# Twenty-four low-half subtracts of weights move from GpSimd to DVE

## The reference, cut to what matters

```
h    = rms_norm(x) ; proj = h @ w_in
y0   = compressed / selected / window attention      (from proj)
y1   = stick-breaking attention                      (from proj)
y2   = gated linear attention, 4 heads               (from proj)
y3   = forgetting attention: softmax(q k^T + cum_q - cum_k), 8 heads, from fox_q, fox_k, fox_v
x    = x + (sum_n sigmoid(gates_n) * (y_n @ w_branch_n)) @ w_out
x    = x + relu(rms_norm(x) @ w_ff1)^2 @ w_ff2
```

## Time and profile before

| | |
|---|---|
| median of 3 runs | 3802.38 us |
| lowest and highest | 3798.88 and 3803.84 us |
| profiled execution, its own time | 3799.13 us |
| span of its profile | 3797.8 us |
| TensorE matmul busy | 3651.8 us (96%) |
| DVE busy | 2161.4 us (57%) |
| ScalarE busy | 1305.7 us (34%) |
| GpSimd busy | 1197.6 us (32%) |
| mean granted TensorE clock | 0.978 |

### The profile page before, as it was taken

How to read it: one execution, slowest core, us unless ns; L and a number is a source line. 1 busy time by engine, 2 the same in 40 slices (tenths; PEclk the granted TensorE clock), 3 DMA queues, 4 the chain that set the end, 5 groups by cost and what they waited for, 6 DMA issues and landing times.

```text
span 3797.8 us, 44671 instructions
## 1 busy us (share of the span) xinstructions
PE 3651.8 (96%) x17862; PEld 2808.5 (74%) x17862; DVE 2161.4 (57%) x3054; ACT 1305.7 (34%) x2217; POOL 1197.6 (32%) x486
## 2 busy tenths in 40 slices
PE   8889999998999999999999999999999999999998
PEld 6646888865588888676777678887767777778887
DVE  7787565688754474633374485545553255365445
ACT  6344121443522131544423532123354433342212
POOL 0002444200144443132333244444213232334443
PEclk9889999997999999999999999999999999999999
DMA  4101333320033333121222123334112222223332
GB/s 135 43 12 50 98 96 95 93 68 12 23 95 99 95 119 107 39 68 56 78 62 78 51 90 99 95 98 148 51 40 78 57 78 61 67 73 95 99 95 83
DMA packets 81373, 292.38 MB, mean 77 GB/s; under 512 B 9712, under 2 KB 11152, under 8 KB 80656
## 3 DMA queue, kind: packets, MB, share of 16 engines
q1 hardware_dynamic: 78384, 278.49, 24.0%
q10 hardware_dynamic: 2784, 11.03, 0.9%
HBM read 285.30 MB, written 2.10 MB: 76 GB/s over the span
## 4 chain that ended last, share of the span: by engine, by line
PE 85%; DVE 11%; issue 2%; ACT 2%; DMA 0%; SPq 0%; DVEq 0%; ACTq 0%
PE acc L334 23%; PE acc L336 22%; PE acc L335 22%; PE banks L929 2%; PE banks L648 2%; PE banks L604 2%; DVE conv_c L1307 2%; PE banks L631 2%; PE banks L940 1%; DVE stat L728 1%; PE banks L1555 1%; DVE probs L739 1%; DVE QK L857 1%; DVE w_lo L247 1%; DVE pair L406 1%
## 5 line engine op out<-in xcount | busy, mean ns | idle before, releaser
L278 POOL TENSOR_TENSOR w_lo<-w_raw,w_hi 128x1024 fp32r<-128x1024 f32 x482 | 1197.4, 2485 | 2570.1 <-ACT w_hi L231 2570.1
L231 ACT ACTIVATE w_hi<-w_raw 128x1024 fp32r<-128x1024 f32 x518 | 548.9, 1060 | 1725.5 <-PE acc L336 1641.6
L334 PE MATMUL acc<-hH,w_hi 128*128 128x512 f32 x1776 | 730.9, 412 | 13.2 <-DVE sig L1940 6.6
L336 PE MATMUL acc<-hL,w_hi 128*128 128x512 f32 x1776 | 699.4, 394 | 0.0
L335 PE MATMUL acc<-hH,w_lo 128*128 128x512 f32 x1776 | 698.8, 393 | 0.0
L334 PEld LDWEIGHTS acc<-hH,w_hi 128*128 128x128 f32 x1776 | 337.9, 190 | 99.7 <-issue 25.3
L334 PE MATMUL acc<-H,w_hi 128*128 128x512 f32 x1024 | 400.4, 391 | 3.8 <-DVE L L398 3.8
L369 DVE TENSOR_TENSOR xT<-acc,xT 128x512 f32<-128x512 f32 x160 | 110.7, 692 | 514.1 <-PE acc L336 495.6
L334 PE MATMUL acc<-midH,w_hi 128*128 128x512 f32 x1024 | 400.3, 391 | 0.3
L335 PE MATMUL acc<-midH,w_lo 128*128 128x512 f32 x1024 | 398.5, 389 | 0.0
L336 PE MATMUL acc<-midL,w_hi 128*128 128x512 f32 x1024 | 398.5, 389 | 0.0
(11 more groups left out here) (325 smaller groups left out, 4710.7 us busy)
## 6 DMA issues: line engine op xcount, KB each, us to landing
w_raw<-in_stream SPq DMA_DIRECT2D x518, 512.0 KB, 3.6
cw<-in_cmpw ACTq DMA_DIRECT2D x2, 2048.0 KB, 7.4
mixed<-in_cmpw ACTq DMA_DIRECT2D x2, 2048.0 KB, 12.7
x_tok<-in_x SPq DMA_DIRECT2D x2, 1024.0 KB, 7.4
out<-f_tok SPq DMA_DIRECT2D x8, 256.0 KB, 2.1
stack<-Z ACTq DMA_DIRECT2D x8, 128.0 KB, 2.3
stack<-Z ACTq DMA_DIRECT2D x8, 127.8 KB, 2.4
masks_f<-in_masks SPq DMA_DIRECT2D x1, 960.0 KB, 12.0
```

The costliest lines, as they stand in the source:

```text
L231: act.activation(w_hi[:, u % WB, 0:w], w_raw[:, u % 2, 0:w], ACT.Copy).then_inc(hi_split, 1)
L278: pool.tensor_tensor(w_lo[:, u % WB, 0:w], w_raw[:, u % 2, 0:w], w_hi[:, u % WB, 0:w], ALU.subtract)\
L334: pe.matmul(acc[n % 2][:, :], wh, H[:, k, :], start=(k == 0), stop=False)
L336: last = pe.matmul(acc[n % 2][:, :], wh, Lo[:, k, :], start=False, stop=(k == nk - 1))
```

## The change

DVE makes the low parts of the units of `fox_in` too, where the index `j` is 2 or more. In `evacuate`, the subtract is issued only behind the last tile of a unit.

```diff
         def by_dve(u):
-            layer, j, group, _, _, _ = UNITS[u]
-            return layer < DEPTH and j >= 2 and group in ("first_in", "late_in")
+            _, j, group, _, _, _ = UNITS[u]
+            return group in ("first_in", "late_in", "fox_in") and j >= 2
...
                 for _ in range(len(self.tiles) if count is None else min(count, len(self.tiles))):
-                    u, _, n = self.tiles.pop(0)
+                    u, t, n = self.tiles.pop(0)
                     dve.wait_ge(acc_ready[n % 2], n // 2 + 1)
                     take(n - self.first, acc[n % 2], acc_free[n % 2], n // 2 + 1)
-                    if u + 2 < len(UNITS) and by_dve(u + 2):
+                    if t == UNITS[u][4] - 1 and u + 2 < len(UNITS) and by_dve(u + 2):
                         split_lo_dve(u + 2)
```

## The result

The changed kernel takes 3807.82 us (median of 22 runs, 3801.50 to 3812.01) against 3801.62 for the kernel before on the same chip. The ratio is 1.0015, 95% interval 1.0009 to 1.0022: by that ratio some 5.7 us slower. The forecast was 3801.6 us, no measurable change, with a range up to 3807.0. It was wrong: the kernel is slower, clear of the noise, and its time lies above the range. The profiled execution took 3808.49 us.

A forecast was written before the change was run, and what follows sets the result against it. TensorE, with 85% of the chain, was taken as the bound, so DVE's work counts only where TensorE waits. 2 x (-0.7 + 0.7 - 0.4 + 0) = -0.8 us from the median 3802.38 gave 3801.6 us, range 3796.5 to 3807.

The forecast's parts named there:

- Bound and mechanism: Around fox_in, TensorE bounds the chain; its idle stretches end with DVE instructions, some held about 2 us by GpSimd's subtracts.
- Term 1: Steady steps behind evacuations: DVE's added subtract fits the slack of 0.71 and 0.32 us before L929, so 0.
- term 5: Late in the fox_in stage: unit 11's DVE subtract overlaps GpSimd's first `mix2` subtract before QK; taken as 0, +1.0 otherwise.
- The steps' rival: Steps behind evacuations lose their slack if DVE's subtract takes 1.9 us or more; 3817.6 us at 2.41; chance 0.05.
- Term 2: Start of the fox_in stage: first L929 comes sooner, limited by unit 3's later load and ScalarE's copy; -0.7 us a layer.
- Term 3: End of run 0: the subtract delays masked copy L885, which TensorE's value matmuls wait for; +0.7 us a layer.
- a new slow stretch: Before the value matmuls, 2.1 us idle lowers TensorE's clock, 1.7 us a layer on top; 3805.0 us; chance 0.15.
- Term 4: Behind the copies of two heads: subtract adds 1.21 us, the gap no longer held saves 1.65; -0.4 us a layer.
- slow stretch with term 5 against me: Lower TensorE clock behind the value matmuls' wait, plus QK held by GpSimd late in the stage: 3807.0 us.

The follow-up runs named there:

- run 0: Not a follow-up kernel: a part of the recurrence within the fox_in stage of each second-type layer, ending with masked copy L885 and TensorE's value matmuls; no time of its own.

## Why the prediction was wrong

**Bound and mechanism: right.** The hold-ups of DVE were GpSimd's subtracts, and went with them. All twelve units of a layer moved, as the index said. The DVE subtract took 1.21 us.

**Term 1, the steady steps: right.** Apart from the meeting of term 5, no idle time stands before the L929 behind an evacuation in the steady steps, in either layer: the slack of 0.71 and 0.32 us held. The steps' rival is out.

**Term 2, the front: right in mechanism, a little low in size.** -0.7 us was forecast for the first L929. It starts at 1913.80 with the stage 1.0 us late, against 1913.92: -1.1; over the six layers of three profiles it is -0.7 to -1.1. The load, ScalarE's copy and the exponentials were the chain, each within 0.7 us of the forecast. The idle time before it is 2.5 to 3.0 us where 3.2 was forecast. Behind it, a slow stretch follows in all six layers of the changed kernel, in four of six of the kernel before, so that part of the gain is paid back. Whether the change causes that difference is open.

**Term 3, the end of run 0: right as a delay, wrong as a whole.** This is the step that failed. It was priced at the delay itself, +0.7 us, and measured +0.6; but the rival "a new slow stretch", held at 0.15, is what happened. The idle time of 2.0 us lay between the 1.41 that the trace showed to be harmless and the 2.44 that it showed to be dear, and I put it with the harmless. It costs 2.2 us a layer by the profile, 4.4 in all; 4.9 to 6.8 by the ratios of the pairs with and without it. So a penalty of 1.6 us a layer was put at nothing in the sum. The error was to keep it as a rival at 0.15 when the rows left open, between those two values, where idle time begins to cost.

**Term 4, the head copies: right.** -0.4 forecast, -0.5 measured.

**Term 5, the meeting: wrong.** I took 0, from the row at 1928.38; it is +0.8 us a layer, near the upper bound of 1.0. The row was misread. DVE's timeline of the kernel before shows what it left out:

```profile
1928.39 0.69 DVE L857 TENSOR_TENSOR QK<-Z,gap 128x512 f32<-128x512 f32 x1
...
1929.63 2.26 DVE L848 TENSOR_TENSOR gap<-cum 128x512 f32<-128x512 f32 x1
```

There GpSimd asked at 1928.38, just as QK was being issued; its 2.96 us are 0.55 of waiting and 2.41 of work, so it waited about as long as QK took and no longer. QK was not held, it seems because it was the instruction under way; the next gap, at 1929.63, was (2.26 us in place of 0.68). Behind a subtract of 1.21 us, GpSimd asks in its middle and gets in at its end, ahead of what DVE has queued. The rule of the Trainium skill that I set beside the row ("SBUF — State Buffer", section "Who interferes with whom") was the better guide: by it, the sum would have been 2 us higher, and 1.6 were measured.

**The sum.** With the terms as measured, 2 x (-0.9 + 2.2 - 0.5 + 0.8) = +3.2 us, and about 4.0 with the allowance for the front made above. The forecast's own case "slow stretch with term 5 against me" said 3807.0, and 3807.82 was measured. That closeness is in part luck: the stage gives 4.0 of the 5.7 us, and the other 1 to 2 us lie outside it. The three profiled executions of the changed kernel are longer than those of the kernel before by 9.1 us in the mean, of which 3.7 are slow stretches near 1520 and 2705 us. These differ between executions of the same kernel; that the changed kernel has more of them is what three profiles of each show, not something I can explain.

Three details of the prediction do not hold either. Its sentence that a change under 7.6 us can't be told from none was too coarse: some 20 runs of each kernel told 5.7 us from none. The lower end of its range, 3796.5, is 0.3 us below what its own terms add up to. And a subtract of 1.9 us, named as one that breaks the cover of every step, would be 0.69 us longer, which is just under the slack of 0.71.

## What to carry to other kernels

Freeing an engine from another's hold-ups gains only what the critical engine waited for, while each instruction put ahead of a critical one costs twice where the wait it makes is long enough for TensorE's clock to fall (here 2.0 us, and not 1.3 to 1.6): where a row leaves open whether an idle time is harmless, price both. When work is moved to another engine, look at each place where the critical engine waits for a short chain (here L885 and the value matmuls) and issue the moved work behind it, not ahead; and look at what the moved work releases (here a load in whose shadow another engine's queue stood). Two instructions a layer moved by a few us made of a loss of 0.15% a gain of 0.22%.

## What was not expected of the hardware

- Whether the granted clock falls behind an idle time of TensorE is not a matter of its length alone. In the 14 profiles, from 1450 to 3700 us, a slow stretch came within 6 us behind none of 93 idle times of 1.28 to 1.64 us, behind nine of ten of 2.02 us, behind both of 2.5 us at the end of run 0, behind 13 of 22 of 2.4 to 3.0 us at the front of the stage, and at 23 of 26 of 3.3 us ahead of `mix2`. Each costs about 1.6 us, and the totals step by that: +1.6, +3.2, +4.8.
- The same program, the kernel before, loses 0, 1.7 or 4.9 us near 2705 us, with TensorE never idle there, in three executions (granted clock 1.00, 0.91 and 0.74 over 20 us).
- A GpSimd subtract that finds a DVE instruction under way begins when that one ends, ahead of the next in DVE's queue: it took 2.89 us in place of 2.41 at 1992.42, and the QK behind took 2.90 in place of 0.69. The same pair of 2.9 us stands at 1944.59 with unit 7 on GpSimd and at 1987.42 with unit 11.
